# Recurrent stage of a two-block transformer kernel: projection with both halves of x in one moving operand, sums on VectorE, first convolution tap on ScalarE

## What is computed

```python
def rglru_mixer(x, w_in, conv_w, conv_b, w_a, b_a, w_x, b_x, a_param, w_out):
    z = x @ w_in                                   # 1024 -> 2 * 1280
    gate_branch, xb = z[..., :D_RNN], z[..., D_RNN:]
    xp = jnp.pad(xb, ((0, 0), (CONV_WIDTH - 1, 0), (0, 0)))
    xc = conv_b + conv_w[0] * xp[:, 0:S]
    for k in range(1, CONV_WIDTH):                 # CONV_WIDTH = 4
        xc = xc + conv_w[k] * xp[:, k:k + S]
    r = sigmoid(per-head xc @ w_a + b_a)
    ig = sigmoid(per-head xc @ w_x + b_x)
    log_a = -8 * r * softplus(-a_param)
    a = exp(log_a); mult = sqrt(-expm1(2 * log_a))
    h = scan over tokens of h = a * h + mult * (ig * xc)
    return (h * gelu(gate_branch)) @ w_out         # 1280 -> 1024
```

## Time and profile before

| what | value |
|---|---|
| time, median of 3 runs | 1763.2 us (1761.23 to 1763.4) |
| time of the profiled execution | 1761.19 us |
| its span in the profile | 1759.4 us |
| TensorE matmul busy | 1738.7 us, 99% |
| VectorE, ScalarE busy | 1268.5 us, 1003.5 us |
| granted TensorE clock | 1.00 in every stretch that was read |

### The profile page before, as it was taken

The page is one execution under the profiler, slowest core; times in us unless marked ns, Lnnn a source line. Parts: engine busy times, 40 slices in busy tenths (PEclk is TensorE's granted clock), DMA queues, the critical chain, the costliest instruction groups (busy, mean ns, idle before and its releaser), DMA issues.

```text
span 1759.4 us, 26008 instructions
## 1 busy us (share of the span) xinstructions
PE 1738.7 (99%) x10391; PEld 1544.4 (88%) x10391; DVE 1268.5 (72%) x1608; ACT 1003.5 (57%) x1263; POOL 62.3 (4%) x94
## 2 busy tenths in 40 slices
PE   8999999999999999999999999999999999999998
PEld 7888998888888888888889999888888999988887
DVE  5766777766677666866667988867667998877665
ACT  6544657654467445644467766465446966555444
POOL 7300000000000000000001000000000000000000
PEclk9999999999999999999999999999999999999999
DMA  9765535665545655365545544356554554356652
GB/s 232 245 191 191 168 120 168 213 217 191 190 166 191 198 191 189 122 215 191 191 158 176 184 152 136 120 184 226 187 190 159 168 168 135 129 167 198 191 188 92
DMA packets 230103, 311.76 MB, mean 177 GB/s; under 512 B 6594, under 2 KB 203076, under 8 KB 229892
## 3 DMA queue, kind: packets, MB, share of 16 engines
q1 hardware_dynamic: 225904, 303.84, 53.5%
q0 software_dynamic: 3792, 6.43, 1.3%
q10 hardware_dynamic: 324, 0.34, 0.1%
HBM read 309.54 MB, written 1.05 MB: 177 GB/s over the span
## 4 chain that ended last, share of the span: by engine, by line
PE 91%; DVE 4%; ACT 3%; issue 1%; DMA 0%; SPq 0%; ACTq 0%; DVEq 0%
PE psD L1866 28%; PE psA L1795 27%; PE psA L1800 14%; PE psA L1848 6%; PE psA L1749 4%; PE psA L1853 3%; PE psA L1754 2%; PE psA L1866 2%; PE psD L2140 1%; DVE lo L903 1%; PE psD L2077 1%; PE psD L1931 1%; PE psA L1931 1%; DVE xT L936 1%; ACT hi L445 1%
## 5 line engine op out<-in xcount | busy, mean ns | idle before, releaser
L903 DVE TENSOR_TENSOR lo<-raw,hi 128x2048 fp32r<-128x2048 f32 x285 | 650.7, 2291 | 175.1 <-ACT hi L445 174.4
L445 ACT ACTIVATE hi<-raw 128x2048 fp32r<-128x2048 f32 x285 | 542.2, 1908 | 68.9 <-PE psD L1866 33.5
L1795 PE MATMUL psA<-xT,hi 128*128 128x512 f32 x2102 | 504.7, 391 | 2.9 <-DVE xT L936 2.9
L1795 PEld LDWEIGHTS psA<-xT,hi 128*128 128x128 f32 x2102 | 388.3, 188 | 81.9 <-DVE xT L936 5.5
L1800 PEld LDWEIGHTS psA<-xT,lo 128*128 128x128 f32 x2112 | 271.9, 191 | 11.0
L1800 PE MATMUL psA<-xT,lo 128*128 128x256 f32 x2112 | 276.2, 283 | 0.0
L1866 PE MATMUL psD<-hi,prod_hi 128*128 128x512 f32 x544 | 173.5, 393 | 3.0 <-issue 3.0
L1866 PE MATMUL psD<-hi,prod_lo 128*128 128x512 f32 x544 | 171.9, 390 | 0.0
L1848 PE MATMUL psA<-hi,xT 128*128 128x256 f32 x1152 | 146.3, 285 | 0.0
L1848 PEld LDWEIGHTS psA<-hi,xT 128*128 128x128 f32 x1152 | 140.5, 192 | 2.7 <-issue 2.7
L1866 PE MATMUL psD<-lo,prod_hi 128*128 128x512 f32 x544 | 142.3, 389 | 0.0
(11 more groups left out here) (294 smaller groups left out, 1795.2 us busy)
## 6 DMA issues: line engine op xcount, KB each, us to landing
raw<-in_w_in SPq DMA_DIRECT2D x48, 1024.0 KB, 5.2
raw<-in_ffn_w_up SPq DMA_DIRECT2D x43, 1024.0 KB, 5.3
raw<-in_ffn_w_gate SPq DMA_DIRECT2D x43, 1024.0 KB, 5.4
raw<-in_ffn_w_down SPq DMA_DIRECT2D x43, 1024.0 KB, 5.1
raw<-in_w_gate SPq DMA_DIRECT2D x22, 1024.0 KB, 5.4
raw<-in_w_up SPq DMA_DIRECT2D x22, 1024.0 KB, 5.4
raw<-in_w_down SPq DMA_DIRECT2D x22, 1024.0 KB, 4.9
raw<-in_lru_w_in SPq DMA_DIRECT2D x10, 1024.0 KB, 5.1
```

The costliest lines, as they stand in the source:

```text
L445: act.activation(hi[:, n % RING, :], raw_of(n), ACT.Copy).then_inc(hi_ready, 1)
L903: dve.tensor_tensor(lo[:, n % RING, :], raw_of(n), hi[:, n % RING, :].bitcast(F32), ALU.subtract).then_inc(lo_ready, 1)
L1795: pe.matmul(psA[:, bank + f, :], w_hi[:, k, f * P:(f + 1) * P], xT[:, k].rearrange("p e s -> p (e s)"), start=(k == 0), stop=False)
```

## The change

The projection of the recurrent stage goes over to `feature_pairs`. Its blocks use two sets of two banks in turn, `psA[:, 0:2]` and `psA[:, 2:4]`, so block `i` waits until block `i - 2` has been summed. ScalarE copies the upper columns of each block to a new place in SBUF (`L_LOW`), VectorE adds the lower ones (`summed_rows`) and multiplies by the row in SBUF (`evacuate`). The first tap of the convolution, a multiplication and the bias, moves from VectorE to ScalarE (`first_tap`), one turn later, and `convolve` moves one turn later too.

```diff
 (ScalarE)
+                    def first_tap(j):
+
+                        act.wait_ge(xb_ready, j + 1)
+                        for ft in (2 * j, 2 * j + 1):
+                            act.activation(view(L_XC, RT, S)[:, ft, :], view(L_XB, RT, S + 3)[:, ft, 0:S], ACT.Identity,
+                                           bias=lru_c[:, 0, ft:ft + 1], scale=conv_w[:, 0, ft:ft + 1]).then_inc(tap_ready, 1)
...
                         if i == half + 3:
                             recurrent_decay(1)
                         n += 1
+                        act.wait_ge(block_used, n)
+                        act.activation(view(L_LOW + 512 * (i % 2), 2, S), psA[:, 2 * (i % 2):2 * (i % 2) + 2, S:2 * S], ACT.Copy).then_inc(row_l_ready, 1)
+                        if 1 <= i <= half:
+                            first_tap(i - 1)
                         if i == half:
 (VectorE)
+                    def summed_rows(i):
+
+                        to = xb[:, 2 * i:2 * i + 2, 3:S + 3] if i < half else gelu[:, 2 * (i - half):2 * (i - half) + 2, :]
+                        dve.wait_ge(row_l_ready, i + 1)
+                        dve.tensor_tensor(to, psA[:, 2 * (i % 2):2 * (i % 2) + 2, 0:S], view(L_LOW + 512 * (i % 2), 2, S), ALU.add).then_inc(row_summed, 1)
+
                     def evacuate(i):
 
-                        dve.wait_ge(block_used, n + 1)
-                        rows_in(i)
...
+                        to = xb[:, 2 * i:2 * i + 2, 3:S + 3] if i < half else gelu[:, 2 * (i - half):2 * (i - half) + 2, :]
+                        row = rrow[:].unsqueeze(1).broadcast_to([P, 2, S])
+                        dve.wait_ge(row_summed, i + 1)
+                        dve.tensor_tensor(to, to, row, ALU.mult).then_inc(xb_ready if i < half else gate_in, 1)
...
-                        for ft in fts:
-                            step(dve.tensor_scalar(xc[:, ft, :], xb[:, ft, 0:S], conv_w[:, 0, ft:ft + 1], lru_c[:, 0, ft:ft + 1], ALU.mult, ALU.add))
+                        dve.wait_ge(tap_ready, 2 * (i + 1))
...
                             split_to(n + 1)
-                            dve.wait_ge(block_used, n + 2)
-                            rows_in(2 * half - 1)
+                            summed_rows(2 * half - 1)
+                            evacuate(2 * half - 1)
...
                         if i == 0:
+                            summed_rows(0)
                             norm_stats()
+                        if 1 <= i < 2 * half - 1:
+                            summed_rows(i)
                         if i == 1:
                             take_row()
                             evacuate(0)
-                            convolve(0)
                         if 1 <= i < 2 * half - 1:
                             evacuate(i)
-                        if 1 <= i < half:
-                            convolve(i)
+                        if 1 <= i <= half:
+                            convolve(i - 1)
 (TensorE)
-                        if 4 <= i < 4 + half:
-                            pe.wait_ge(xb_ready, i - 3)
-                        elif i >= 4 + half:
-                            pe.wait_ge(gate_in, i - 3 - half)
-                        features(n + 1, n, psA[:, i % 4, :], fresh=(i == 0))
+                        if i >= 2:
+                            pe.wait_ge(row_summed, i - 1)
+                        feature_pairs(n + 1, n, 2 * (i % 2), fresh=(i == 0))
```

More of the change, by code:

```diff
@@ L73 @@
 QK_T = GATE_B
+L_LOW = BAND + 2 * 2 * GT * 384
 SQUARES, TURNER = 22016, 22528
 SCRATCH = 22784
-assert BAND + 2 * 2 * GT * 384 <= SCRATCH
+assert L_LOW + 2 * 512 <= SQUARES
 def head_pieces():
@@ L159, in build @@
         query_evac = sem("query_evac")
+        row_l_ready, row_summed, tap_ready = sem("row_l_ready"), sem("row_summed"), sem("tap_ready")
         gate_l_ready, up_l_ready, gate_summed, up_summed = sem("gate_l_ready"), sem("up_l_ready"), sem("gate_summed"), sem("up_summed")
```

## The result

| | before | after |
|---|---|---|
| median over 11 runs each | 1762.28 us | 1767.86 us |
| range | 1760.81 to 1764.75 | 1765.23 to 1772.27 |
| profiled execution, its span | 1761.19, 1759.4 us | 1765.23, 1763.4 us |

The ratio is 1.0031, with a 95% interval of 1.0022 to 1.0040: the change makes the kernel slower by 5.6 us in the medians. The profiled execution of the changed kernel is the fastest of its eleven.

What follows compares the result with a forecast made beforehand. TensorE, with 91% of the chain, was taken to bound the kernel. Gain -2.0 against waits 1.7, 1.4 and 3.2 sums to 4.3, by clock times +4.7 us, taken from median 1763.2 to 1767.9 us; range 1763.5 to 1770.5.

Steps and rivals of the forecast that it cites:

- Gain of 0.20 a block: TensorE's projection blocks: 16 matmuls of 512 replace 16 pairs of 256, 5.56 us against 5.76; ten blocks give -2.0 us.
- Wait at `row_of_scales`, 1.7: Stage start: VectorE's sum of block 0 waits for ScalarE's copy ahead of its statistics, so TensorE stands 1.7 us.
- No wait at blocks 4 and 5, 0.4 of slack at block 5: VectorE's turn of 6.29 us exceeds a block's 5.56, but sums arrive 1.1 and 0.4 us before TensorE wants the banks.
- Wait at tile 9, 1.6: Gates: ScalarE's copy of block 6 delays its table load and chain by 2.0 us; tile 9 starts at 264.3, TensorE stands 1.6.
- Wait at block 12, 3.2, total +4.7: Tail: copies of blocks 7 and 8 delay VectorE's second recurrence; low half 7.6 us later, TensorE stands 3.2, total +4.7 us.
- rival of the clock (C): Behind block 12's wait the clock halves to 1.2 GHz for a block, costing 5.5 us more: 1773 us; chance 0.07.
- Rival A: Not slower: the tail stays covered, low half for block 12 less than 3.0 us later; +1.4 us, 1764.6; chance 0.23.
- Rival B: Slower: VectorE's pace binds, turns 0.4 us longer make TensorE wait about 1 us at block 5; 1769 us; chance 0.10.

Runs made afterwards that it cites:

- the four kernels that lost most of the waits: Changed kernel with: statistics and copies reordered, 0.9996; also block 8's splits late, 1.0003; also an early product, 0.9993; or new form in blocks 0 to 5 only, 1.0001.

## Why the prediction came out, point by point

**Gain of 0.20 a block.** Right: 5.57 from block to block. The rule for an isolated matmul in the Trainium skill ("TensorE: Matmul & The Clock Gate", section "Back-to-back issue gap"), by which I had worked out 0.4 us for all ten blocks, does not carry over to this stream, as the same rows show.

**Wait at `row_of_scales`, 1.7.** 1.59, by the order that was named (VectorE waits 2.39 for the copy, then makes its statistics). Shown by swapping the two: the wait goes, 1.25 us come back.

**No wait at blocks 4 and 5, 0.4 of slack at block 5.** Right: the sum of block 3 ended at 229.74 (229.06 and 0.68) and block 5 began at 230.32, 0.6 later. The slack is small, since both an earlier block 2 (statistics first) and the tap's return made it a wait (0.32 and 0.16).

**Wait at tile 9, 1.6.** 1.71. Moving the copy of block 6 took 0.66 of it away; leaving that copy out, with blocks 6 to 9 in the old form, took it to the 0.21 of before.

**Wait at block 12, 3.2, total +4.7.** 2.76 and +4.49 up to block 12, +4.68 for the stage. The mechanism is shown from both sides: copies moved, the wait is gone (-3.1 us); one more operation in front, the wait grows by 0.95 and block 12 is 1.00 later. The 0.4 that the wait is shorter comes from both ends, by the stage's own clock: the recurrence began 0.3 sooner than forecast (87.90 from its start; 283.63 - 195.43 is 88.20), and TensorE came to block 12 0.2 later (98.60, where 293.8 - 195.43 is 98.37).

**The total.** The forecast of 1767.9 beside a measured 1767.86 is closer than its working deserves; that is luck. The part that was mis-sized is the rival of the clock (C). I gave it a chance of 0.07 and a price of 5.5 us, because the one row at hand showed 3.0 us without work and no fall. In six profiles of kernels with the wait of 2.76 us (the changed kernel three times, and three variants) it fell in five, and the stretch from block 12 to the next norm then took 15.1, 15.2, 15.35, 15.4 and 16.65 us in place of 13.8: 1.3 to 2.9 us. So C's chance was far too low and its price too high by a factor of two to four. An execution with a fall has 4.7 from the waits and some 1.5 from the clock, 6.2; one without has 4.7. The medians differ by 5.6 in the first set and by 6.3 in the second; in how many of the executions without a profile the clock fell at block 12 is not known. My number hit because the median that I started from, 1763.2 of 3 runs, was 0.9 above the 1762.28 of 11. The Trainium skill's sentence that throttled is the resting state and activity releases it ("TensorE: Matmul & The Clock Gate", "Part 1: The HAM clock gate") agrees with these rows (0.50 behind the pause, 1.00 again 3 to 6 us after TensorE had resumed); I had weighed it too lightly against one execution.

**Rival A** did not come about: the low half for block 12 was 7.3 us later by the stage's own clock (100.62 from its start against 93.34), not less than 3.0. Its price was about right: it gave +1.4 with the tail covered and the early waits left, and the kernel with the two copies moved has +1.59 in its stage. **Rival B** is refuted: TensorE never waited for a sum in the changed kernel.

## What to carry to other kernels

When a short operation is put into an engine's list, ask not only what it costs. Ask what stands in front of it, and what is queued behind the operation that waits for it. Ten copies of 0.6 us, each harmless by its length, made the stage 4.7 us longer net by three places in two lists. A wait of the bounding engine of nearly 3 us costs more than its length, since the clock may fall behind it, and one profile doesn't tell how often it does. And a gain of 0.2 us a block is worth what the tightest chain beside it lets through: in the four kernels that lost most of the waits, 0.3 to 0.45 of the 2.0 us arrived.

## What was not expected of the hardware

- **The clock behind a pause.** It fell behind the pause of 2.76 us at block 12 in five profiles of six and behind 3.71 in the one. Behind 1.5 to 1.75 in this stage (`row_of_scales`, tile 9, block 12 in the variant with only the copy of block 7 moved) it fell in none. All kernels have a pause near 38 us, in the first feed-forward. In the 14 profiles it never fell there behind pauses of 1.48 to 1.91 us (five), fell in three of six with 2.72 to 3.02 us, and in all three with 3.40 to 4.74 us. So the length of the pause alone doesn't decide: a pause of 3.02 us passed without a fall in the profile of before (3.0 in the earlier trace rows), while the clock fell behind one of 3.02 in the third profile of the changed kernel. Its pause, and its busy time by stretches with the granted clock:

```profile
38.35 0.82 PE L1879 MATMUL psD<-hi,prod_hi 128*128 128x512 f32 x2 [3.02 <-issue]
...
36.00:40.00 4.00, 1.65 (x5) 1.34 (x6) 3.31 (x4) 2.49 (x3) 4.00 (x9) 0.85 0.20 44
40.00:44.00 4.00, 4.00 (x15) 3.20 (x14) 2.44 (x4) 1.36 (x3) 4.00 (x9) 0.73 0.59 172
```

Nor are the short ones always harmless. In the first profile of the changed kernel the clock fell to 0.50 from 12 to 14 us, behind a pause of 1.56; in the other 13, with pauses of 0.97 to 1.61 us at that place, it stayed at 1.00. What else decides stays open.
- **Where executions of one kernel differ.** The pause near 38 us was 1.48, 3.02 and 4.74 us in the three profiles of the changed kernel, and the recurrent stage began at 195.04, 197.37 and 199.55. With stages of 115.15, 118.06 and 116.49 us that is nearly all of the difference between 1765.23, 1770.78 and 1771.15.
- **A block behind a wait is slower by 0.1 to 0.2 us** under full clock: 3.92 to 3.96 for the high part in place of 3.82 (3.79 at block 12). The wait may not be the cause: behind the gates' matmuls, without a wait of TensorE, the high part of block 6 took 4.00 (246.92 in the changed kernel), and 4.18 in place of 4.00 in the kernel before. No run tells the two apart.
- **The tap with scale and bias by partition** from SBUF takes 1.09 us for two of 128x256, ScalarE's tanh of that shape 0.90 by my estimate from the earlier trace rows.
